# One contiguous 16 KB row per partition for the expert weights of a two-block transformer kernel

## The reference, cut to what matters

```python
def expert_block(args):
    xb, e = args
    u = xb @ w1[e] + b1[e]
    glu = jnp.minimum(u[:, ::2], SWIGLU_LIMIT)
    lin = jnp.clip(u[:, 1::2], -SWIGLU_LIMIT, SWIGLU_LIMIT)
    a = glu * jax.nn.sigmoid(SWIGLU_ALPHA * glu) * (lin + 1.0)
    return a @ w2[e] + b2[e]
```

## Time and profile before

| | us |
|---|---|
| median of 3 runs | 2023.46 (2023.11 to 2023.74) |
| span of the profiled execution | 2019.0 |
| PE busy | 1908.6 (95%) |
| DVE busy | 692.9 (34%) |
| ACT busy | 596.1 (30%) |
| POOL busy | 115.7 (6%) |
| the SP queue's transfers, share of 16 DMA engines over the span | 71.7% |

### The profile page before, as it was taken

The page is one execution under the profiler, slowest core; times in us unless marked ns, Lnnn a source line. Parts: engine busy times, 40 slices in busy tenths (PEclk is TensorE's granted clock), DMA queues, the critical chain, the costliest instruction groups (busy, mean ns, idle before and its releaser), DMA issues.

```text
span 2019.0 us, 27425 instructions
## 1 busy us (share of the span) xinstructions
PE 1908.6 (95%) x11143; PEld 1256.9 (62%) x11144; DVE 692.9 (34%) x1163; ACT 596.1 (30%) x987; POOL 115.7 (6%) x94
## 2 busy tenths in 40 slices
PE   7999989989989899999799999999999999999996
PEld 6666668979988799889754444444444444444343
DVE  1111224669974644446412122122212112112112
ACT  2344357465544455555300001010000000000012
POOL 1000000036630000000000000000000000000000
PEclk9999999999999999999879999999999999999998
DMA  4322324488964654434749999999999999999992
GB/s 163 125 84 90 119 84 147 158 290 308 308 224 147 189 182 147 167 112 171 287 180 410 419 418 417 418 418 417 418 418 417 418 418 418 418 419 417 418 377 105
DMA packets 182033, 568.25 MB, mean 281 GB/s; under 512 B 5521, under 2 KB 77305, under 8 KB 149041
## 3 DMA queue, kind: packets, MB, share of 16 engines
q1 hardware_dynamic: 180560, 561.97, 71.7%
q0 software_dynamic: 1408, 5.38, 1.0%
HBM read 566.26 MB, written 3.43 MB: 282 GB/s over the span
## 4 chain that ended last, share of the span: by engine, by line
PE 61%; DMA 25%; DVE 6%; ACT 4%; issue 3%; SPq 1%; DVEq 0%; ACTq 0%
DMA s_ring<-in_w_mlp 25%; PE banks L1973 13%; PE banks L1621 10%; PE banks L1631 6%; PE banks L1632 6%; PE banks L1633 6%; PE banks L2008 4%; PE banks L1983 3%; DVE r_wl L1217 2%; PE banks L1963 1%; PE banks L1566 1%; PE banks L1750 1%; PE banks L2022 1%; PE banks L1751 1%; PE banks L1752 1%
## 5 line engine op out<-in xcount | busy, mean ns | idle before, releaser
L1973 PE MATMUL banks<-s_ring,s_W 128*64 128x512 f32 x2048 | 462.7, 599 | 20.2 <-DMA s_ring<-in_w_mlp 13.9
L1973 PEld LDWEIGHTS banks<-s_ring,s_W 128*64 128x64 f32 x2048 | 143.0, 137 | 301.5 <-issue 262.4
L1475 DVE TENSOR_TENSOR s_W<-banks,s_W 128x512 f32<-128x512 f32 x128 | 82.1, 683 | 608.4 <-PE banks L1963 608.4
L2008 PE MATMUL banks<-s_ring,s_W 128*64 128x512 f32 x1024 | 226.4, 594 | 0.3 <-ACT s_W L1026 0.3
L1621 PE MATMUL banks<-s_W,s_ring 128*128 128x256 f32 (+1 forms) x768 | 179.9, 391 | 4.6 <-DVE s_W L1074 4.6
L1621 PEld LDWEIGHTS banks<-s_W,s_ring 128*128 128x128 f32 x768 | 146.1, 193 | 33.6 <-issue 10.5
L2008 PEld LDWEIGHTS banks<-s_ring,s_W 128*64 128x64 f32 x1024 | 76.1, 138 | 144.7 <-issue 144.1
L1286 DVE TENSOR_TENSOR r_w2l<-s_ring,r_w2h 128x1024 fp32r<-128x1024 f32 x96 | 116.9, 1223 | 86.2 <-ACT r_w2h L895 86.0
L1031 ACT ACTIVATE s_W<-banks 128x512 f32<-128x512 f32 x32 | 19.1, 597 | 422.7 <-PE banks L2008 422.7
L1631 PE MATMUL banks<-r_x2h,r_w2h 128*128 128x256 f32 x448 | 131.2, 293 | 6.1 <-DVE r_x2l L1300 6.1
L1983 PEld LDWEIGHTS banks<-s_W 128*128 128x128 f32 x1024 | 123.2, 200 | 13.5 <-issue 11.4
(11 more groups left out here) (375 smaller groups left out, 2894.6 us busy)
## 6 DMA issues: line engine op xcount, KB each, us to landing
s_ring<-in_w_mlp SPq DMA_DIRECT2D x192, 2048.0 KB, 20.8
s_ring<-in_w_in SPq DMA_DIRECT2D x38, 1024.0 KB, 4.9
s_ring<-in_w_in SPq DMA_DIRECT2D x12, 2048.0 KB, 7.9
s_ring<-in_w_ada SPq DMA_DIRECT2D x12, 2048.0 KB, 8.1
s_ring<-in_w_ffn_gate SPq DMA_DIRECT2D x11, 1024.0 KB, 5.3
s_ring<-in_w_ffn_up SPq DMA_DIRECT2D x11, 1024.0 KB, 7.9
s_ring<-in_w_ffn_down SPq DMA_DIRECT2D x5, 2048.0 KB, 7.8
s_ring<-in_w_gate SPq DMA_DIRECT2D x4, 2048.0 KB, 7.9
```

Of the source, the lines that this page charges most:

```text
L1973: last = mm(pb[b][64 * h:64 * h + 64, :], XgT[:, 2 * c + k, :], slot(c, 2)[:, k, 1024 * h + 512 * b:1024 * h + 512 * b + 512], start=c == ...
L2008: last = mm(pb[2][64 * h:64 * h + 64, :], aT[:, k, 64 * c:64 * c + 64], slot(4 + c, 4)[:, k, 512 * h:512 * h + 512], start=c == 0 and k == ...
```

## The change

The rows that a partition takes of a chunk now lie together. For `w1`, `"(p k) n -> p (k n)"` gives partition p the rows 2p and 2p + 1 of the chunk, and for `w2` the rows 4p to 4p + 3: one piece of 16 KB of memory for each partition, in both. So row block k of a chunk now holds rows 2p + k (4p + k), and what meets it is permuted to match:

- ACT's four copies into `htok` (L1011 before) read as before but write column 2p + k of each 256 to place 128k + p. Two neighbouring elements go to places 512 bytes apart.
- DVE's reads of `u` (L1493, L1494) take every eighth float (a step of 32 bytes) in eight runs of 64, and write `gl` and `li` without gaps, in the order (k, bank, row).

The instructions of every engine, their number and their order are the same as before, and so is the number of DMAs (192 loads of expert weights). Some semaphores were joined: pairs that are raised one after the other now share a name and count on (`sb_scores` and `df_scores` are `scores`, `log_mm` and `rank_mm` are `route_mm`, `df_max` and `dl_max` are `row_max`, `df_exp` and `dl_e` are `row_exp`, `vec_turned` is the sixth of `x_turned`). The rounds for an expert with more than 64 tokens (`again`, `next_round`) are changed in the same way; the 192 loads in the profile are 6 for each of 32 experts, so those rounds don't run on these inputs.

```diff
         for c in range(3):
-            sp.dma_start(slot(c, 2), w1[0, T * c:T * c + T, :].rearrange("(k p) n -> p k n", p=P)).then_inc(inw[c], 16)
+            sp.dma_start(ring[:, c, :], w1[0, T * c:T * c + T, :].rearrange("(p k) n -> p (k n)", p=P)).then_inc(inw[c], 16)
 
 
         def first(e, c):
-            sp.dma_start(slot(c, 2), w1[bass.ds(e, 1), T * c:T * c + T, :].rearrange("e (k p) n -> p (e k) n", p=P))\
+            sp.dma_start(ring[:, c, :], w1[bass.ds(e, 1), T * c:T * c + T, :].rearrange("e (p k) n -> p (e k n)", p=P))\
               .then_inc(inw[c], 16)
 
         def second(e, c):
-            sp.dma_start(slot(4 + c, 4), w2[bass.ds(e, 1), 512 * c:512 * c + 512, :].rearrange("e (k p) n -> p (e k) n", p=P))\
+            sp.dma_start(ring[:, 4 + c, :], w2[bass.ds(e, 1), 512 * c:512 * c + 512, :].rearrange("e (p k) n -> p (e k n)", p=P))\
               .then_inc(inw[4 + c], 16)
...
-        act.wait_ge(S["vec_turned"], 1)
+        act.wait_ge(S["x_turned"], 6)
...
             act.wait_ge(S["ht_mm"], b + 1)
-            act.activation(htok[:, b // 2, 512 * (b % 2):512 * (b % 2) + 512], pb[4 + b], ACT.Copy).then_inc(S["ht_kept"], 1)
+            half = htok[:, b // 2, 512 * (b % 2):512 * (b % 2) + 512]
+            act.activation(half.rearrange("q (c k p) -> q c p k", c=2, k=2), pb[4 + b].rearrange("q (c p k) -> q c p k", c=2, k=2),
+                           ACT.Copy).then_inc(S["ht_kept"], 1)
...
+        def u_half(c):
+
+            return banks[:, 0:2, :].rearrange("p a (q k c) -> p k a q c", k=4, c=2)[:, :, :, :, c]
+
+        def by_row(buf):
+
+            return buf.rearrange("p (k a q) -> p k a q", k=4, a=2)
...
                 dve.wait_ge(S["u_mm"], e * 5 + 5)
                 since(dve, "a_done", e)
-                u = banks[:, 0:2, :].rearrange("p a (n c) -> p a n c", c=2)
-                ts(gl.rearrange("p (a n) -> p a n", a=2), u[:, :, :, 0], 7.0, None, ALU.min)
-                ts(li.rearrange("p (a n) -> p a n", a=2), u[:, :, :, 1], 7.0, -7.0, ALU.min, ALU.max).then_inc(S["u_read"], 1)
+                ts(by_row(gl), u_half(0), 7.0, None, ALU.min)
+                ts(by_row(li), u_half(1), 7.0, -7.0, ALU.min, ALU.max).then_inc(S["u_read"], 1)
```

More of the change, by code:

```diff
@@ L387, in program @@
         "x_in", "vec_in", "cst_in", "lam_in", "tab_in", "hot_in", "toep_out", "toep_in", "moe_in", "b1_in", "stored",
[L388 removed]
+        "x_turned", "x_kept", "vec_kept", "filled", "lam_sum", "lam_exp", "csil",
         "norm_sq", "norm_ms", "norm_r", "norm_x", "norm_s",
@@ L586, in _ @@
         sp.wait_ge(S["gemm2"], len(GR2))
-        sp.dma_start(slot(3, 2), w1[0, 3 * T:4 * T, :].rearrange("(k p) n -> p k n", p=P)).then_inc(inw[3], 16)
+        sp.dma_start(ring[:, 3, :], w1[0, 3 * T:4 * T, :].rearrange("(p k) n -> p (k n)", p=P)).then_inc(inw[3], 16)
         def load(e, w2_too=True):
@@ L737, in sb_step @@
             if s == "sbA":
-                act.wait_ge(S["sb_scores"], h + 1)
+                act.wait_ge(S["scores"], h + 1)
                 if h:
@@ L758, in df_step @@
             if s == "dfA":
-                act.wait_ge(S["df_max"], h + 1)
+                act.wait_ge(S["row_max"], h + 1)
                 for qt in range(2):
@@ L764, in df_step @@
                                               accum_out=sml[:, 20 + 2 * qt + c:21 + 2 * qt + c])
-                last.then_inc(S["df_exp"], 1)
+                last.then_inc(S["row_exp"], 1)
             if s == "dfB":
@@ L947, in dl_step @@
             if s == "dlE":
-                act.wait_ge(S["dl_max"], h + 1)
+                act.wait_ge(S["row_max"], HEADS + h + 1)
                 for qt, v in enumerate((ds[:, 0:384], ds[:, 384:1152])):
                     last = act.activation(v, v, ACT.Exp, bias=sml[:, 16 + qt:17 + qt], accum_out=sml[:, 18 + qt:19 + qt])
-                last.then_inc(S["dl_e"], 1)
+                last.then_inc(S["row_exp"], 1)
             if s == "dlB":
@@ L1149, in df_step @@
             if s == "dfA":
-                dve.wait_ge(S["df_scores"], h + 1)
+                dve.wait_ge(S["scores"], HEADS + h + 1)
                 for c in range(2):
@@ L1158, in df_step @@
                 st.wait()
-                ts(sml[:, 16:20], sml[:, 16:20], -1.0, None, ALU.mult).then_inc(S["df_max"], 1)
-                dve.wait_ge(S["df_exp"], h + 1)
+                ts(sml[:, 16:20], sml[:, 16:20], -1.0, None, ALU.mult).then_inc(S["row_max"], 1)
+                dve.wait_ge(S["row_exp"], h + 1)
                 st.do(nc.vector.reciprocal(sml[:, 24:28], sml[:, 20:24]))
@@ L1379, in dl_step @@
                 st.wait()
-                ts(sml[:, 16:18], sml[:, 16:18], -1.0, None, ALU.mult).then_inc(S["dl_max"], 1)
+                ts(sml[:, 16:18], sml[:, 16:18], -1.0, None, ALU.mult).then_inc(S["row_max"], 1)
             if s == "dlN":
-                dve.wait_ge(S["dl_e"], h + 1)
+                dve.wait_ge(S["row_exp"], HEADS + h + 1)
                 st.do(nc.vector.reciprocal(sml[:, 20:22], sml[:, 18:20]))
@@ L1418, in _ @@
         dve.wait_ge(S["moe_in"], 48)
-        dve.wait_ge(S["log_mm"], 1)
+        dve.wait_ge(S["route_mm"], 1)
         st.do(tt(lg, pb[1][:, 0:2 * E].rearrange("p (a e) -> p a e", a=2), bc(brow, 2), ALU.add))
@@ L1449, in _ @@
         dve.sem_inc(S["route"], 1)
-        dve.wait_ge(S["rank_mm"], 1)
+        dve.wait_ge(S["route_mm"], 2)
         st.do(stt(rank[:, :, 0:E], pb[0][:, 0:2 * E].rearrange("p (a e) -> p a e", a=2), 1.0, msk, ALU.add, ALU.mult))
@@ L1522, in next_round @@
         def next_round(r):
+            dve.wait_ge(S["round"], r)
             ts(taken, taken, float(CAP), None, ALU.add).then_inc(S["round"], 1)
@@ L1536, in again @@
             dve.wait_ge(S["over_pe"], n * 7 + 4)
-            u = banks[:, 0:2, :].rearrange("p a (n c) -> p a n c", c=2)
-            ts(gl.rearrange("p (a n) -> p a n", a=2), u[:, :, :, 0], 7.0, None, ALU.min)
-            ts(li.rearrange("p (a n) -> p a n", a=2), u[:, :, :, 1], 7.0, -7.0, ALU.min, ALU.max).then_inc(S["over_dve"], 1)
+            ts(by_row(gl), u_half(0), 7.0, None, ALU.min)
+            ts(by_row(li), u_half(1), 7.0, -7.0, ALU.min, ALU.max).then_inc(S["over_dve"], 1)
             dve.wait_ge(S["over_dve"], n * 7 + 3)
@@ L1589, in _ @@
         pe.wait_ge(S["vec_in"], 16 * len(VEC_ROWS))
-        nc.tensor.transpose(pb[5][:, 0:NVEC], vrow, ident[0:NVEC, 0:NVEC]).then_inc(S["vec_turned"], 1)
+        nc.tensor.transpose(pb[5][:, 0:NVEC], vrow, ident[0:NVEC, 0:NVEC]).then_inc(S["x_turned"], 1)
         def group(GR, g, w, x, sem_name, evacs):
@@ L1668, in sb_step @@
                 mm(pb[3][:, T:384], skT[:, h, M + P:TM], q[:, P:T], start=True, stop=True)
-                mm(pb[4][0:M, 0:T], skT[:, h, 0:M], q, start=True, stop=True).then_inc(S["sb_scores"], 1)
+                mm(pb[4][0:M, 0:T], skT[:, h, 0:M], q, start=True, stop=True).then_inc(S["scores"], 1)
             if s == "sbB":
@@ L1703, in df_step @@
                                   dkT[v, h, 0:144 + P * qt], start=True, stop=True)
-                last.then_inc(S["df_scores"], 1)
+                last.then_inc(S["scores"], 1)
             if s == "dfB":
@@ L1942, in _ @@
                 last = mm(pb[1][:, E * t:E * t + E], hn[:, k, P * t:P * t + P], wr[:, k, :], start=k == 0, stop=k == KT - 1)
-        last.then_inc(S["log_mm"], 1)
+        last.then_inc(S["route_mm"], 1)
         turn_back("ht_mm", None)
@@ L1949, in _ @@
         mm(pb[0][0:1, 2 * E:3 * E], ones[:, 0:1], msk[:, 0, :], start=True, stop=False)
-        mm(pb[0][0:1, 2 * E:3 * E], ones[:, 0:1], msk[:, 1, :], start=False, stop=True).then_inc(S["rank_mm"], 1)
+        mm(pb[0][0:1, 2 * E:3 * E], ones[:, 0:1], msk[:, 1, :], start=False, stop=True).then_inc(S["route_mm"], 1)
         for t in range(2):
```

8 lines of the change are left out of this document (4 added, 4 removed).

## The result

The changed kernel takes **2004.0 us** (median of 4 runs, 2003.6 to 2004.9) against 2023.6 (4 runs, 2023.1 to 2023.7): a ratio of 0.991, with a 95% interval of 0.9896 to 0.9923. The gain of 19.6 us is far outside the scatter of either kernel, which is 1.3 us at most in these runs. The forecast was 2004.5, in a range of 2003.5 to 2024.5. The profiled execution has a span of 2002.6 us.

The account below looks back on a forecast made before the run. DMA was taken to bound the later experts, PE's own beat the earlier ones. Span 2019.0 - 19.4 (faster loads, limited by PE) + 0.4 (ACT's copies) = 2000.0, plus 4.46 to the median: 2004.5 us, range 2003.5 to 2024.5.

Parts of the forecast that it names:

- Two regimes, and DMA as the bound of the second: Expert stage: PE sets a beat of 29.38 us up to expert 13, DMA one of 30.43 from expert 14.
- The account of a round: One expert's six weight chunks take 30.12 us, the bias through one engine 0.31 more: the beat of 30.43.
- The check over 30 rounds: From SP's issue to the landing of expert 31's chunk 3: 915.35 us = 30 x 30.43 + 2.45 for starting up.
- The cost of a packet: Expert weight loads: each packet costs an engine 10.1 ns; 80 fewer a round save 0.81 us, making it 29.62.
- The cap: End of expert stage: PE's own beat of 29.38 us limits the gain to 19.4 us, not 24.
- DVE's reads: L1493 and L1494, reading PSUM with a step of 32 bytes: 0 cost; bounds up to +1.05 us an instruction.
- ACT's copies: L1011, four copies into htok writing neighbours 512 bytes apart: +0.4 us, bounds 0 and 1.6.
- Length above 8 KB gives nothing: Expert weight loads: 16 KB rows bring no gain, beat stays at 30.43, kernel 2023.9 us; chance 0.12.
- part of it: Expert weight loads: only a third of the 10.1 ns belongs to packets, round 30.16, kernel 2015.8 us; chance 0.08.
- Longer pieces make DMA slower: Expert weight loads: all six chunks at 409 GB/s, round 31.08 us, kernel 2043.4 us; chance 0.05.
- DVE as the new bound: L1493, L1494: slower reads lengthen PE's beat; 2020 us at +0.52 each (chance 0.03), slower kernel from +0.58, 2052.6 at +1.05 (0.10).
- The step from span to time: Whole kernel: the median of the runs lies 4.46 us above the profiled span, so 2000.0 becomes 2004.5.

Follow-up runs that it names:

- Experiment 5: Kernel before the change with half of the matmuls of u left out, w1 in 8 KB and w2 in 4 KB rows: 2010.4 us, one run.
- experiment 3: Kernel before the change without the 8 KB bias load of each expert after the first: 2014.9 us, ratio 0.9962 to the kernel before.
- experiment 4: Changed kernel with htok permuted where ACT reads PSUM (step of two floats) and written without gaps: 2002.7 us.
- experiment 1: Changed kernel with w2's loads and DVE's reads put back, so only w1 has 16 KB rows: 2014.6 us, ratio 0.996 to the kernel before.
- experiment 6: Changed kernel, all rows 16 KB, with half of the matmuls of u left out: 1988.4 us, one run.
- experiment 7: Kernel before the change with half of the matmuls of u left out and w2 also in 8 KB rows: 2003.7 us, one run.
- experiment 8: Kernel before the change with half of the matmuls of u left out and w1 also in 4 KB rows: 2031.6 us, one run.
- experiment 11: Changed kernel with both of DVE's reads of u made a second time into spare space: 2020.7 us, ratio 0.9992 to the kernel before.
- experiment 2: Changed kernel with w1's loads and the copies into htok put back, so only w2 has 16 KB rows: 2007.7 us, ratio 0.9932 to the kernel before.

## Why the prediction was right, step by step

- **Two regimes, and DMA as the bound of the second.** Right. Experiment 5, with PE's work cut, keeps the beat of 30.42.
- **The account of a round** (30.12 for the chunks, 0.31 for the bias). Right in both sizes: experiment 3 took the bias out and the late beat fell by 0.31. It is not right for every round. Up to expert 9 the landings are 30.1 apart, bias or not, and the other fifteen engines do not wait for the one with the bias.
- **The check over 30 rounds.** It closed partly by luck. The 2.45 us "for starting up" were the remainder, not a measurement. By the semaphore events the first round took 35.19 us, 4.8 more than 30.43, and the rounds up to expert 10 gave 2.3 back. The forecast could use the sum all the same, since the changed kernel starts in the same way: from its issue at 1061.13 to the last chunk 3 at 1954.36 are 30 x 29.68 + 2.8.
- **The cost of a packet.** 10.1 ns forecast, 9.4 measured. It came from two rates read to 1 GB/s, and 9.4 lies inside the bounds given (8.5 to 11.6). The round became 29.68 instead of 29.62. That made no difference, as anything below 29.78 reaches the cap; it would have been a miss of 30 x 0.06 = 1.8 us had PE not been there.
- **The cap.** Right, and the step that made the number. 29.38 holds to expert 31, whose chunk 3 has landed at 1954.36 when PE starts on it at 1957.13. So DMA was ahead by 2.8 us at the end, where 5 were forecast. The stretches that DMA ruled lost 18.4 + 0.9 = 19.3 us against 19.4. Without the cap, the sum would have said 24 (or 30 x 0.75 = 22.5 at the measured round).
- **DVE's reads.** 0 forecast, 0 measured. A step of 32 bytes costs no more than one of 8, so the rule of 8-byte lines in the Trainium skill ("Advanced Engine Details and Errata", section "PSUM Cachelines"), which the prediction applied to DVE as a possible price, has no price for DVE's reads in this kernel.
- **ACT's copies.** +0.4 forecast, +0.5 measured in the trace, on the write side (experiment 4).
- **The rivals.** "Length above 8 KB gives nothing" and "part of it" fell to experiments 1 and 6 to 8: six row plans, one line. With the second falls the estimate of 3.5 ns worked out from the Trainium skill ("DMA: Bandwidth & Descriptors", section "Why small descriptors are slow (HBM only)"); the measured 9.4 ns is nearly three times that. "Longer pieces make DMA slower" fell with the round of 29.68. DVE as the new bound needed 0.58 us more for each read and got none; by experiment 11 the point from which it decides lies rather at 0.68 ((19.0 + 29 x 0.79) / 62).
- **Semaphores.** 0 forecast, and both forms beat at 29.38 where PE rules. "No wait is added" holds for the code that runs here; DVE's `next_round`, which doesn't run, has gained one (on `round`).
- **The step from span to time.** Wrong, with no harm. I put the median 4.46 us above the span for good. In every run since, of either kernel, time and span of the same execution differ by 1.8 or 1.9 us (2004.4 and 2002.6, for one). By that, the profiled execution of before was a quick one, some 2.7 us under its median (4.46 - 1.8). Most of that is the start, which is 2.5 us shorter in its trace than in the changed kernel's (first row of the table above). So the runs' time does not hold 4.5 us more than the span, and the span forecast for after (2000.0) was low by as much as it was quick (2002.6 measured). Differences of medians and of single spans should be kept apart: the spans differ by 16.4, the medians by 19.6, and the table above shows which rows of the 16.4 belong to the change.

## What to carry to other kernels

When a stage is bound by transfers, count the packets that each DMA engine moves in one round, multiply, and set the sum beside the beat; if the account closes, it also tells what longer rows will bring. Then find the beat of the next engine, because it caps the gain: here some 22.5 us of transfer time (30 x 0.75) bought 19 us of kernel time. Look also for transfers into one partition in such a stream: by experiment 3, the bias would be worth moving in a form that loads all engines alike while DMA sets the beat. That was not tried, and in the changed kernel, where PE sets the beat, it should bring nothing. A permutation that the loads want is best paid where data is anyway copied with room to spare, on the side that costs nothing, which was the read from PSUM for DVE and for ACT.

## What the runs showed of the hardware that was not expected

- **A packet costs a DMA engine 9.4 ns beside its bytes, whatever its length** from 4 to 16 KB, so that rates go 410, 422, 428 GB/s over the saturated stretch (experiments 8, 7 and 6).
- **A transfer into one partition is a transfer through one engine.** In a stream of full transfers that engine falls behind the others by 0.31 us a round for 8 KB (6.8 us by expert 31), and every full transfer lands with it. The others run ahead, so the rate of the page stays at 418 GB/s and does not show the loss (experiment 3).
- **ACT pays for writes that jump by 512 bytes at every element,** 1.09 us instead of 0.60 for one copy of 512 columns, or about 0.3 us each if the four in a row are taken (3.74 us), and nothing for reads with a step of 8 bytes.
- **SP is held less.** The issue of a `w1` load took up to 8.2 us before and 0.35 at most after. It goes with the 4 KB rows of `w2`, not with the number of packets: 8.0 us in experiment 1 (96 packets, `w2` in 4 KB), 0.39 at most in experiments 2 and 7 (80 and 96 packets, none of 4 KB). No wait in the traces of before and after is put down to it.
- **In experiments 5 to 8 a few beats are 1.7 us too long,** each followed, at once or some rounds later, by one that is 1.7 too short. From expert 20 to 31, over which the rounds above were averaged, they cancel, and the beats between them are the plain ones (30.43, 29.68, 30.14 and 31.03). What does it stays open; no run was made for it.
